# One kernel, three expert gathers: each gather entered by its first token tile alone, and row requests of the second block moved

## The reference, cut to what matters

```python
def _modulate(x, g, shift, scale):
    return _rmsnorm(x, g) * (1 + scale) + shift

def _peer(h, w_pq, peer_keys, peer_down, peer_up):
    q = (h @ w_pq).reshape(B, L, PEER_HEADS, 2, PEER_QDIM // 2)
    s = jnp.einsum("blhpd,hpkd->blhpk", q, peer_keys)
    sv, si = lax.top_k(s, PEER_TOPK)
    cand = (sv[..., 0, :, None] + sv[..., 1, None, :]).reshape(B, L, PEER_HEADS, 256)
    cidx = (si[..., 0, :, None] * N_KEYS + si[..., 1, None, :]).reshape(B, L, PEER_HEADS, 256)
    top_s, pos = lax.top_k(cand, PEER_TOPK)
    eidx = jnp.take_along_axis(cidx, pos, axis=-1)
    gate = jax.nn.softmax(top_s, axis=-1)
    def one(hh, ee, gg):                      # 128 tokens
        a = jnp.einsum("tkd,td->tk", peer_down[ee], hh)
        return jnp.einsum("tk,tkd->td", gg * jax.nn.gelu(a), peer_up[ee])

# each layer
mix_x, _ = _token_mix(h, ...)                 # ends in  (gated sum) @ w_out
x = x + m_x[2] * mix_x
h2 = _modulate(x, norm2_g[l], m_x[3], m_x[4])
x = x + m_x[5] * _peer(h2, w_pq[l], peer_keys[l], peer_down[l], peer_up[l])
```

## Time and profile before

| | us |
|---|---|
| median of 3 runs | 4588.42 |
| the runs | 4582.87, 4588.42, 4593.35 |
| the profiled execution | 4584.24 |
| its span, first to last instruction | 4582.4 |

### The profile page before, as it was taken

One profiled execution on the slowest core, in us unless ns is written; L12 is line 12 of the kernel. 1 busy time (PEld: TensorE's weight loads), 2 busy tenths in 40 slices (PEclk: granted clock), 3 DMA queues, 4 the chain that ended last, 5 costly groups with the idle time before them and its releaser, 6 DMA issues.

```text
span 4582.4 us, 34528 instructions
## 1 busy us (share of the span) xinstructions
PE 3426.4 (75%) x10470; PEld 1705.2 (37%) x10470; DVE 2582.4 (56%) x5497; ACT 832.1 (18%) x1972; POOL 2029.9 (44%) x2148
## 2 busy tenths in 40 slices
PE   6888686898677689767868766766768876876667
PEld 3356442465233246311344222211356644422111
DVE  1312677456777644766346774676453336665766
ACT  1311112222111121111311111111232111111111
POOL 0210466555566555665216663565000004666665
PEclk8899799999789899755989997756769987999556
DMA  5663799999999889999859998998100027998999
GB/s 208 215 214 145 267 365 321 356 374 402 358 375 344 308 310 387 365 367 349 284 188 350 361 366 320 403 393 334 67 1 1 1 92 263 343 367 338 379 360 351
DMA packets 379743, 1328.13 MB, mean 290 GB/s; under 512 B 39484, under 2 KB 44860, under 8 KB 375976
## 3 DMA queue, kind: packets, MB, share of 16 engines
q0 software_dynamic: 313344, 1141.10, 66.6%
q1 hardware_dynamic: 60064, 162.08, 9.7%
q10 hardware_dynamic: 6152, 22.74, 1.3%
HBM read 1324.59 MB, written 1.17 MB: 289 GB/s over the span
## 4 chain that ended last, share of the span: by engine, by line
PE 17%; POOL 11%; DMA 9%; issue 8%; DVE 6%; ACT 1%; another core or an unknown queue 1%; DVEq 0%; POOLq 0%; ACTq 0%
PE ps L1491 16%; POOL arena L2767 11%; DMA arena<-in_peer_up,arena 4%; DVE arena L747 3%; DVE arena L760 2%; DMA arena<-in_peer_v,arena 1%; DMA arena<-in_peer_u,arena 1%; DMA arena<-in_peer_down,arena 1%; ACT arena L2194 1%; PE ps L1497 1%; DMA arena<-in_ada_w 1%; ACT L2194 0%; DVE arena L768 0%; DVE arena L1103 0%
## 5 line engine op out<-in xcount | busy, mean ns | idle before, releaser
L1491 PE MATMUL ps<-arena 128*128 128x512 f32 (+11 forms) x9732 | 3310.7, 523 | 938.3 <-ACT arena L2194 242.0
L1491 PEld LDWEIGHTS ps<-arena 128*128 128x128 f32 (+5 forms) x9732 | 1605.7, 198 | 2568.9 <-issue 1992.3
L760 DVE SCALAR_TENSOR_TENSOR arena<-arena,ps 128x1024 f32<-128x1024 f32 x1024 | 1239.1, 1217 | 472.9 <-DMA arena<-in_peer_down,arena 242.4
L2767 POOL DMA_INDIRECT arena<-in_peer_down,arena x768 | 738.8, 962 | 795.4 <-DVE arena L764 307.1
L2767 POOL DMA_INDIRECT arena<-in_peer_up,arena x768 | 737.3, 960 | 509.0 <-PE ps L1491 235.1
L2194 ACT ACTIVATE arena<-arena 128x128 f32<-128x128 f32 (+5 forms) x1250 | 448.7, 384 | 2117.2 <-issue 610.4
L2767 POOL DMA_INDIRECT arena<-in_peer_u,arena x256 | 243.9, 953 | 734.5 <-DVE arena L764 645.1
L760 DVE SCALAR_TENSOR_TENSOR ps<-arena,ps 128x512 f32<-128x512 f32 x508 | 383.1, 754 | 134.4 <-DMA arena<-in_peer_up,arena 65.6
L2194 ACT ACTIVATE arena<-ps 128x512 f32<-128x512 f32 (+3 forms) x381 | 196.6, 516 | 1123.3 <-PE ps L1491 635.7
L747 DVE TENSOR_TENSOR arena<-ps,arena 128x512 f32<-128x512 f32 (+3 forms) x192 | 131.3, 684 | 344.9 <-PE ps L1491 295.5
L2767 POOL DMA_INDIRECT arena<-in_peer_v,arena x256 | 243.4, 951 | 163.1 <-issue 64.2
(11 more groups left out here) (34 smaller groups left out, 566.5 us busy)
## 6 DMA issues: line engine op xcount, KB each, us to landing
arena<-in_w_mod POOLq DMA_DIRECT2D x40, 1024.0 KB, 5.8
arena<-in_gate_blocks SPq DMA_DIRECT2D x16, 2048.0 KB, 8.6
arena<-in_w_in SPq DMA_DIRECT2D x14, 2048.0 KB, 7.9
arena<-in_w_pq SPq DMA_DIRECT2D x12, 2048.0 KB
arena<-in_ada_w POOLq DMA_DIRECT2D x24, 1024.0 KB, 6.0
arena<-in_w_out SPq DMA_DIRECT2D x8, 2048.0 KB, 8.3
arena<-in_gate_blocks SPq DMA_DIRECT2D x8, 1792.0 KB
arena<-mod_scratch ACTq DMA_DIRECT2D x26, 512.0 KB
```

What stands on the lines that cost most here:

```text
L760: self.e.scalar_tensor_tensor(o, a, s, b, op0, op1, accum_out=accum).then_inc(*(inc or self.inc(self.S.vec)))
L1491: return self.e.matmul(o, l, r, start=start, stop=stop)
L2767: self.e.indirect_dma_start(out=o, out_offset=None, in_=table, in_offset=bass.IndirectOffsetOnAxis(ap=idx.bitcast(U32), axis=0)).then_inc( ...
```

## The change

The three entries become one stage, `enter`. It projects, norms, turns and queries tile 0 alone, up to its first pick; the first bank of tile 1's projection is given to PE before tile 0's turns, the second after its key products; tile 1's norm is split over gaps in the pick (`norm_mean`, and `norm_finish` behind the release of POOL). The rest of the queries is woven into the gather tile by tile, with 128 columns moving. Block 0 of the query weights is kept for tile 1 in a place of its own (`consts`) in the second and third entry, and loaded once more in the first. The constants of the second block are therefore loaded later (`second_consts` after the last pick). The rows of an entry's norm are asked for earlier. In the third entry the first half of w_out is loaded during the recurrence (`out_first`), and `close` is split by tile. `second_asked` asks for the second block's rows at step 133 of the gather, and `second_vectors` uses them at step 142.

```diff
-SLOTS = {"three": [0, 1, 2], "two": [0, 1], "third": [2]}
+SLOTS = {"three": [0, 1, 2], "two": [0, 1], "third": [2], "consts": [3], "early": [4]}
...
+    def enter(self, l, MX, HT, m, QA, home, costs=None):
+
+        q, a, p, d, g = costs or (1.0,) * 5
+        front = self.rings["front"]
+        ty = m["tmp"].rearrange("p a b -> p (a b)")
+        self.out_weights(l)
+        if l != 1:
+            self.query_weights(l, 0, home)
+        if l == 2:
+            self.entry_rows(l, self.K.A["norm2_g_2"][0])
+            self.close_tile(0)
+        for c in range(2):
+            self.project_tile(l, 0, c, MX)
+        if l == 2:
+            self.close_tile(1)
+        self.entry_vectors()
+        for c in range(2):
+            self.project_add(0, c, ty)
+        self.norm_squares(0)
+        self.norm_mean(0)
+        self.norm_finish(0)
+        self.project_tile(l, 1, 0, MX)
+        yield from self.norm_turn(0, HT, front)
+        self.project_add(1, 0, ty)
+        yield from self.query(0, 0, HT, QA, None, home == "third")
+        self.fence()
+        yield from self.peer_first(l, 0, m, QA, 0)
+        self.project_tile(l, 1, 1, MX)
+        self.project_add(1, 1, ty)
+        self.norm_squares(1)
+        pick = self.peer_pick(l, 0, m, 0, 2, lambda: self.norm_finish(1))
+        for _ in range(6):
+            yield next(pick)
+        self.norm_mean(1)
+        yield from pick
+        self.query_weights(l, 1)
+        yield from self.at(q, self.query(0, 1, HT, QA, None, False))
+        yield from self.at([p] + 5 * [d], self.peer_first(l, 0, m, QA, 1))
+        yield from self.at(g, self.peer_pick(l, 0, m, 2, 4))
+        yield from self.at(a, self.norm_turn(1, HT))
+        yield from self.at(q, self.query(1, 1, HT, QA))
+        for blk in (2, 3):
+            self.query_weights(l, blk)
+            yield from self.at(q, self.query(0, blk, HT, QA, None, False))
+            yield from self.at(q, self.query(1, blk, HT, QA))
+        for blk in (2, 3):
+            yield from self.at([p] + 5 * [d], self.peer_first(l, 0, m, QA, blk))
+        yield from self.at(g, self.peer_pick(l, 0, m, 4, 8))
+        if home == "third":
+            self.query_weights(l, 0)
+        yield from self.at(q, self.query(1, 0, HT, QA))
...
-        self.run(mix_rest(0, 0, HTx, HTp))
+        self.entry_rows(0, A["norm2_g"][0])
+        self.run(mix_gates(0, 0, HTx))
         self.slot, self.ring = self.slots["two"], self.rings["back"]
-        queries = self.at(query_costs(3.2, 1.2, 0.7, 0.5), self.peer_q(0, 0, pt, HTp, QA))
+        queries = self.enter(0, QT, HTp, pt, QA, "third", (3.2, 1.5, 1.2, 0.7, 0.5))
...
+            self.query_weights(1, 0, "consts")
+            self.entry_rows(1, A["norm2_g"][1])
             yield from self.attend(4, att_bufs(area((BG, BG + 2048), (L1E, NB))), QT, [(KTc, VVc), (KTx, VVx)], AT)
             self.fence()
             yield from self.gate_first(1, MX, ga, area((L1E, NB))(256), AT)
-            self.fence()
-            yield from self.project(1, 0, MX, area((L1E, NB))(512))
...
-        self.weave(x_second(), self.modhalf(K.H2R, vectors), 0.65, rings=("five", "few"), slots=("two", "third"))
+        self.weave(x_second(), self.modhalf(K.H2R, vectors), 0.7, rings=("five", "few"), slots=("two", "third"))
...
+            self.second_consts()
             self.second_keys()
             self.second_mu()
+            yield ("after", NEXT + 5)
+            self.second_asked()
+            yield ("after", NEXT + LAG - 4)
+            self.second_vectors()
             yield ("after", NEXT + LAG + 2)
             self.folded(5)
-            self.second_vectors()
             yield from self.second_norm(0)
...
-        self.second_consts()
...
             self.weave(self.steps(bt % 2, bt), preps(bt + 1) if bt < 3 else iter(()), 5.25, rings=("step", "prep"))
-        self.fence()
-        self.ring, self.slot = self.rings["most"], self.slots["two"]
-        self.run(self.close())
-        self.fence()
-        self.ring = self.rings["wide"]
-        self.run(self.project(2, 0, K.HT2, area((BG, NB))(512)))
-        self.fence()
-        self.run(self.modulate(2, A["norm2_g_2"][0], 3, 0, K.HT2))
+            if bt == 2:
+                self.out_first()
         self.fence()
...
+    def norm_finish(self, t):
+        K, S = self.K, self.S
+        _, (n1, gr, _), _, (n3, sh, sh_in) = self.entry
+        self.wait_ge(*self.next(S.norm_root))
+        self.recip(K.small[:, t:t + 1], K.small[:, t:t + 1])
+        self.stt(K.H2[:, t, :], self.X(t), K.small[:, t:t + 1], gr, M, M)
...
+        if meanwhile:
+            meanwhile()
         self.wait_ge(*self.next(S.gate_exp))
...
+    def query(self, t, blk, HT, QA, ring=None, last=True):
+        s = self.wq[blk]
+        w = self.block(s, 512)
+        b = self.asked = self.bank(ring)
+        self.wait_ge(*self.drained(self.turned_in[t]))
+        self.wait_ge(*s.at)
+        self.wait_ge(*self.vacant(b))
+        for j in range(4):
+            for k in range(8):
+                ins = self.mm(b.ap[:, 128 * j:128 * j + 128], w[:, k, 128 * j:128 * j + 128], HT[:, k, 128 * t:128 * t + 128], k == 0, k == 7)
...
+    def out_first(self):
+        self.wait_ge(*self.K.marks["prepared"])
+        self.wait_ge(self.S.state, 7)
+        self.block(self.K.A["w_out_2"][0], 0, 512, self.slots["early"])
```

More of the change, by code:

```diff
@@ L362, in project, with out_weights, entry_rows, entry_vectors @@
         yield from self.units_of(4)
+    def out_weights(self, l):
+        pass
+    def entry_rows(self, l, g):
+        pass
+    def entry_vectors(self):
+        pass
+    def project_tile(self, l, t, c, MX):
+        self.outs[t, c] = self.bank(self.rings["front"])
+    def project_add(self, t, c, ty):
+        pass
+    def norm_squares(self, t):
+        pass
+    def norm_mean(self, t):
+        pass
+    def norm_finish(self, t):
+        pass
+    def out_first(self):
+        pass
+    def norm_turn(self, t, HT, ring=None):
+        for j in range(2):
+            self.turned_in[t] = self.bank(ring)
+            yield
@@ new lines, in query_weights, with close_tile @@
+    def query_weights(self, l, blk, slot="two"):
+        pass
+    def query(self, t, blk, HT, QA, ring=None, last=True):
+        self.asked = self.bank(ring)
+        yield from self.units_of(2)
+    def close_tile(self, t):
+        pass
+    def enter(self, l, MX, HT, m, QA, home, costs=None):
[48 more added lines that the diff above has]
+        yield from self.at(q, self.query(1, 0, HT, QA))
@@ new lines, in norm_turn, with query_weights, query @@
+    def norm_turn(self, t, HT, ring=None):
+        self.wait_ge(*self.next(self.S.modulated))
+        for j in range(2):
+            b = self.turned_in[t] = self.bank(ring)
+            self.wait_ge(*self.vacant(b))
+            self.turn4(b, [(b.ap[:, 128 * i:128 * i + 128], self.K.H2[:, t, 512 * j + 128 * i:512 * j + 128 * i + 128]) for i in range(4)])
+            yield
+    def query_weights(self, l, blk, slot="two"):
+        self.wq[blk] = self.load(slot=self.slots[slot])
+    def query(self, t, blk, HT, QA, ring=None, last=True):
+        s = self.wq[blk]
+        w = self.block(s, 512)
+        b = self.asked = self.bank(ring)
+        self.wait_ge(*self.drained(self.turned_in[t]))
+        self.wait_ge(*s.at)
+        self.wait_ge(*self.vacant(b))
+        for j in range(4):
+            for k in range(8):
+                ins = self.mm(b.ap[:, 128 * j:128 * j + 128], w[:, k, 128 * j:128 * j + 128], HT[:, k, 128 * t:128 * t + 128], k == 0, k == 7)
+            if j == 1:
+                yield
+        ins.then_inc(*self.fill(b))
+        if last:
+            self.mark(("w", s.i, s.n))
+        yield
@@ L1837, in peer_first, with close_tile @@
+    def close_tile(self, t):
+        K, S = self.K, self.S
+        self.wait_ge(*self.next(S.mixed))
+        for j in range(2):
+            b = self.closed_in[t] = self.bank(self.rings["front"])
+            self.wait_ge(*self.vacant(b))
+            self.turn4(b, [(b.ap[:, 128 * i:128 * i + 128], K.MIX[:, t, 512 * j + 128 * i:512 * j + 128 * i + 128]) for i in range(4)])
+    def peer_first(self, l, t, m, QA, blk, ring=None):
         K = self.K
-        b = self.bank()
+        b = self.bank(ring)
+        if self.asked:
+            self.wait_ge(*self.drained(self.asked))
```

247 lines of the change are left out of this document (156 added, 91 removed).

## The result

The changed kernel takes 4594.11 us (median of 12 runs, 4581.45 to 4604.32), the kernel before 4585.6 beside it: a ratio of 1.0021, 95% interval 1.0012 to 1.003. Forecast was 4534, in a range of 4500 to 4568. The kernel didn't get faster, and by the 0.2% of the prediction it stands on the border between no change and slower (the interval lies above 1). The profiled run has a span of 4589.3 us, against 4582.4.

A forecast was written before the change was run, and what follows sets the result against it. Gathers were taken as bound by transfers, and by PE where heavily woven; entries as single chains with DMA hardly used. -80.4 + 28 + 2 + 4.6 - 13.3 + 5.2 = -53.9 us gave 4534 us, range 4500 to 4568.

The forecast's parts named there:

- the entries: Three stretches from last fence to POOL's first indirect load: shorter by 27.5, 23.9 and 29.0 us, 80.4 in all.
- the signs: In the entries: first MAX8 some 34 us after the fence, PE's clock at its higher level, 64 query instructions in about 7 us.
- Rival (4): Entries and gathers: 128-column matmuls do not cost half; change lost from 0.151 us each, 4600 us at 0.160; chance 0.05.
- the rows of the second block: Fold in the second gather: earlier requests and vectors save 13.3 us, rows crossing a full DMA cost 5.2 us.
- What the gathers give back: Tile 1's work woven into the gathers lengthens them by 8, 10 and 10 us, 28 together; bounds nothing and 48.
- The prediction's own sign of being wrong: Among the signs against the forecast: gathers longer by more than 16 us each.
- what is added there counts in full, 8.9 us: Between 2425 and 2470, PE busy 42.5 of 45 us: PE work added there lengthens the gather by 8.9 us.
- Rival (3): Gathers: PE bursts of five queries in a row pin them, 26.3 us each, 79 instead of 28; 4585 us; chance 0.06.
- q(1,0) at 1.1 us: Tile 1's block 0 queries, last in the gather where PE has 23.4 of 89 us free: cost 1.1 us.
- the constants that move out of the entry: Constants of 1796 KB now load in the second gather instead of the entry: 4.6 us at 403 GB/s.
- the wait of 6.66 us for the rows: First entry's wait for the norm's rows: gone, as the rows are asked for ahead of the gates.
- 28 + 2 + 4.6 - 13.3 + 5.2: Gathers: woven work 28, first gather's reloaded query weights 2, constants 4.6, fold wait -13.3, rows across full DMA 5.2 us.

The follow-up runs named there:

- run 1: Changed kernel with key products and first searches of blocks 2 and 3 put between the queries instead of behind all five; ratio 0.9938 to the kernel before.
- run 3: Changed kernel with block 0 of the second layer's query weights and the second entry's norm rows asked for behind gate_first; ratio 0.9987 to the kernel before.
- the best version: Changed kernel with the edits of run 1 and run 3, rates 0.95 and 0.75, and tile 1's queries between tile 0's search units; 4529.77 us, ratio 0.9882.

## Why the prediction was wrong

**Right: the entries.** -82.5 us against -80.4, each within 1.0 us of its forecast, and the signs too: a search 32.9 us behind the fence (34), 64 query instructions in 7.41 us (7), PE's clock granted at 0.98 and 0.99, its higher level. Rival (4), narrow matmuls at 0.151 us or more, is out: 7.41 / 64 is 0.116. One count in the chain was off: a tile's turns are 8 instructions (1.09 us), not 16. The estimate of 0.160 by the Trainium skill, "TensorE: Matmul & The Clock Gate", section "Back-to-back issue gap", doesn't show here.

**Right: the rows of the second block.** The stop at the fold is 3.16 + 6.48 us in place of 20.26, nothing waits for rows, and putting them back costs 7 us where 8.1 was the term. Two rows of POOL there; the burst of projections behind it stayed, at 18.03 us:

```profile
2849.64 0.94 POOL L2976 DMA_INDIRECT arena<-in_peer_down,arena  x1 [6.48 <-DVE arena L858]
2868.61 0.94 POOL L2976 DMA_INDIRECT arena<-in_peer_up,arena  x1 [18.03 <-PE ps L1631]
```

**Wrong: "What the gathers give back", 28 us.** Measured 15.5, 33.3 and 25.8 without the fold's part, 75 us. The first gather as a whole took 1670 to 1683 us in five kernels that don't differ there, but its first 64 steps hardly scatter (184.6 to 185.3 us in them) and hold 11 to 15 us of the loss. The prediction's own sign of being wrong, gathers longer by more than 16 us each, came in the second and third. The step that failed is "what is added there counts in full, 8.9 us": it priced the added PE work and not its place. The amount was nearly right, as PE's groups of query work and key products in steps 0 to 64 of the second gather show. The kernel before comes first, then the changed one: 29.0 + 4.2 us beside 42.5 + 1.2, so 10.5 more.

```profile
L1491 PE MATMUL ps<-arena 128*128 128x256 f32 x128 | 29.0, 378 | 0.0
L1491 PE MATMUL ps<-arena 128*128 128x128 f32 x24 | 4.2, 330 | 5.0 <-ACT arena L2194 5.0
```
```profile
L1631 PE MATMUL ps<-arena 128*128 128x128 f32 x344 | 42.5, 282 | 7.3 <-ACT arena L2383 7.3
L1637 PE MATMUL ps<-arena 128*128 128x128 f32 x8 | 1.2, 273 | 0.0
```

The steps grew by 27.4 us. I read one window of PE, 42.5 of 45 us busy, and took the rest of the schedule as it was. But the change put five queries in one row, where before searches stood between them. The same work with searches between gives back 14.5 of the 27.4 us in the second gather and 6 to 12 in the first, but only 3.1 of the 19.5 in the third, where the rest stays partly open (run 1 has the clock beside it). Rival (3) named this mechanism, with 26.3 us a gather from the ratio at the fold, and had 0.06 as its chance; the second and third gather came out within 7 us of its price. That closeness is partly luck, since the late picks, which it doesn't name, are in the measured sums too. Its "against", that units are fed one a step, was wrong: one query unit a step is already 5.3 us.

**Not seen: the count of units.** The prediction took the rates as enough. Two units more up to step 64 and four up to step 128 made the picks late, and POOL waited 8.57, 8.34, 3.26 and 21.36 us at them, where the kernel before waited 1.47, 2.49, 0.30 and 11.28. This is also where I put q(1,0) at 1.1 us and 6 came: with an eighth of its work those 6 us stay, with other rates the stop goes in the third gather, while the second gets back 2.5 of its 5.9. The kernel before stood in the third gather with a stop of 11.28 us at exactly this place, which would have told that the account had no reserve.

**Not seen: SP's queue ahead of the second entry, 18.9 us.** The sum has the constants that move out of the entry, but nothing for what the two lines ahead of attend do to their neighbours. I listed what the moved loads need, and not whom they pass. SP waits for a fence at the head of its queue and w_oa stands behind it; the rows and weights then compete with loads that are used at once. Moving them back shows 14.2 of the 18.9 us. In the three later versions with that edit the stretch is 71.0 to 72.0 us, against 69.0 and 69.9 with the old program, so 1 to 5 us are open. The weave's rate, 0.7 for 0.65, may be part of them: run 3 only shows that it isn't the cause of the 14.2.

**Not seen: ACT's queue ahead of the first entry, 4.4 us.** The prediction took the wait of 6.66 us for the rows as gone, since "the rows are asked for ahead of the gates", and put the earlier request at nothing. But ACT asks for them in the order of its work, and waited 5.2 us for its own store (283.38 to 288.54) with evictions behind it; PE's wait for ACT there went from 0.68 to 4.67 us. It is no scatter: in the ten profiles with the moved request the fence behind it stands at 302.0 to 307.5 us, in the two with the old program at 300.1 and 299.4. No run moved this request back by itself.

**Open.** What the 1796 KB of constants cost was forecast at 4.6 us and not measured by itself.

With the three larger causes mended (the best version) the kernel stands 54.5 us under the kernel before on the same chip, close to the 53.9 forecast. By the starts of POOL's loads its stretches outside the gathers are 76.6 us shorter than in the kernel before, where the forecast took off 80.4; its gathers are 22.0 us longer (10.0, 8.2 and 3.8), where 28 + 2 + 4.6 - 13.3 + 5.2 = 26.5 was forecast. So the sum described a schedule that the change didn't have. That the totals meet within 1 us is partly luck: two differences of some 4 us cancel, and the raised rates were no part of the forecast.

## What to carry to other kernels

Work moved out of an idle stretch into a woven one has two prices, its amount and its neighbours: list the units in their new order, and look for heavy ones of one engine side by side and for the due time of the next demand. Count units against the rate before trusting it; a stop of POOL at a demand in the kernel before says that there is no reserve. And for each load that is asked for earlier, write down what its engine has to do next and whether the request waits, for a fence or for a store to land, ahead of that.

## What the runs showed of the hardware

A row of 128-column matmuls costs nearly as much inside the gather as in the quiet entry: 328 in 39.4 us of the run at 2427 (0.120 each) beside 64 in 7.41 (0.116), though indirect loads fill the DMA engines in the one and not in the other. And 8.4 MB asked for within 1.4 us went with a DMA share of 1.03 at 394 GB/s in 25 us soon behind them, and with a PE busy for 13.5 us at a granted clock of 0.80. At the same distance from attend's fence the kernel before has 0.78 at 274 GB/s and 21.5 us of PE, and run 3, without those requests, 0.78 at 266 GB/s and 23.0 us: full transfer engines, and the stage slower for it. SP and ACT asked for those bytes, and POOL's loads of the modulation weights paid. The Trainium skill, "DMA: Bandwidth & Descriptors", section "Issuing engines are not separate DMA queues", states that transfers of all issuing engines share the same 16 DMA engines and interleave; the trace agrees, with 18.3 us of PE's waits for in_ada_w where there were 6.4.

```profile
2215.00:2240.00 25.00, 13.45 (x55) 5.76 (x54) 5.58 (x12) 5.51 (x12) 3.32 (x5) 0.80 1.03 394
```
```profile
2222.76:2247.76 25.00, 21.50 (x114) 9.54 (x112) 10.08 (x21) 8.94 (x20) 6.18 (x9) 0.93 0.78 274
```
```profile
2203.90:2228.90 25.00, 23.04 (x134) 10.38 (x131) 9.98 (x20) 9.04 (x20) 6.98 (x10) 1.00 0.78 266
```
